# A decode step of a hybrid decoder on one core: layer norm statistics read from PSUM, and the second output projection gathered into eight split products

## The reference

```
layer 0:  h = rms_norm(x);  a, b, z = split(h @ w_in, 3)      # 3 x 2048 channels
          u = a * sigmoid(b);  c = causal depthwise conv, width 31, + bias
          c = silu(layer_norm(c) )                            # over 2048 channels
          x = x + (c * silu(z)) @ w_out0
          x = x + sigmoid(x @ gate_w[0]) * (p[0] @ ple_w[0])
shared:   k, v, logf from x;  k normed per head; 16 heads of 64
layer 1:  q, z from x;  o = softmax(q k^T + forget bias) v     # prompt: causal over 1024 keys
          x = x + (o * silu(z)) @ w_out                        # decode: 8 x 4096 cached keys by page table
          x = x + sigmoid(x @ gate_w[1]) * (p[1] @ ple_w[1])
```

## Time and profile before

| | |
|---|---|
| device time, median of 3 runs | 2558.25 us (2555.23 to 2560.53) |
| profiled execution, its own time | 2548.34 us, span 2546.5 us, mean TensorE clock 0.954 |
| convolution, layer norm | to 646 us, 646 to 776 us |
| slots | 1683 to 2382 us |
| rest of the projection | 2382 to 2418 us |
| `ple(1)` and the store | 2418 to 2546.5 us |

### The profile page before, as it was taken

The page is one execution under the profiler, slowest core; times in us unless marked ns, Lnnn a source line. Parts: engine busy times, 40 slices in busy tenths (PEclk is TensorE's granted clock), DMA queues, the critical chain, the costliest instruction groups (busy, mean ns, idle before and its releaser), DMA issues.

```text
span 2546.5 us, 44564 instructions
## 1 busy us (share of the span) xinstructions
PE 2284.5 (90%) x15044; PEld 1844.7 (72%) x15044; DVE 1390.6 (55%) x1990; ACT 949.7 (37%) x1622; POOL 1145.8 (45%) x802
## 2 busy tenths in 40 slices
PE   5999999997449998979999899877999999999799
PEld 4999999997249998969888686634454545545399
DVE  4789988899791016566785211023545455454523
ACT  4556655655351013223332121323343443434311
POOL 0798889988563214444445332232232232222211
PEclk7999999999669998989999999988999999999999
DMA  3222222222033121135635788899999999997312
GB/s 110 73 73 67 72 80 64 73 74 70 18 114 123 45 89 53 65 126 163 182 138 182 258 280 295 287 361 365 387 347 349 349 360 363 357 360 277 117 48 81
DMA packets 143702, 464.36 MB, mean 182 GB/s; under 512 B 28001, under 2 KB 36578, under 8 KB 142386
## 3 DMA queue, kind: packets, MB, share of 16 engines
q1 hardware_dynamic: 117954, 384.07, 43.2%
q0 software_dynamic: 22848, 62.56, 7.4%
q10 hardware_dynamic: 2736, 15.60, 1.5%
HBM read 403.58 MB, written 60.65 MB: 182 GB/s over the span
## 4 chain that ended last, share of the span: by engine, by line
PE 53%; POOL 12%; DVE 11%; issue 8%; DMA 8%; ACT 5%; SPq 2%; ACTq 0%; POOLq 0%; DVEq 0%
POOL ACC L1385 7%; PE PS L610 5%; PE PS L608 5%; PE PS L609 5%; PE PS L703 4%; PE PS L826 4%; PE PS L769 4%; PE PS L705 4%; PE PS L704 4%; PE PS L910 4%; DMA KV<-ck 3%; DMA KV<-cv 3%; PE PS L921 2%; PE PS L895 2%; PE PS L616 2%
## 5 line engine op out<-in xcount | busy, mean ns | idle before, releaser
L1358 POOL TENSOR_TENSOR WL<-RAW,WH 128x1024 fp32r<-128x1024 f32 (+1 forms) x113 | 283.6, 2510 | 454.4 <-ACT WH L995 447.9
L1710 DVE SCALAR_TENSOR_TENSOR PS<-UX,CWT,PS 128x1024 f32<-128x1024 f32 (+1 forms) x672 | 466.3, 784 | 0.0
L641 PE MATMUL PS<-HH,WH 128*128 128x384 f32 (+1 forms) x1152 | 378.9, 329 | 20.7 <-DVE HL L1696 20.7
L643 PE MATMUL PS<-HH,WL 128*128 128x384 f32 (+1 forms) x1152 | 377.8, 328 | 0.0
L642 PE MATMUL PS<-HL,WH 128*128 128x384 f32 (+1 forms) x1152 | 377.6, 328 | 0.0
L703 PE MATMUL PS<-GH,WH 128*128 128x384 f32 (+1 forms) x792 | 272.4, 344 | 29.8 <-DVE KC L1820 16.2
L1385 POOL TENSOR_TENSOR ACC<-ACC,PROD 128x1088 f32<-128x1088 f32 x112 | 284.7, 2542 | 31.3 <-ACT PROD L1047 25.1
L705 PE MATMUL PS<-GH,WL 128*128 128x384 f32 (+1 forms) x792 | 263.5, 333 | 0.0
L704 PE MATMUL PS<-GL,WH 128*128 128x384 f32 (+1 forms) x792 | 262.6, 332 | 0.0
L641 PEld LDWEIGHTS PS<-HH,WH 128*128 128x128 f32 x1152 | 217.6, 189 | 24.7 <-issue 13.7
L1602 POOL DMA_DIRECT2D QI<-qX_scr x128 | 77.7, 607 | 326.4 <-PE PS L879 324.9
(11 more groups left out here) (224 smaller groups left out, 4667.8 us busy)
## 6 DMA issues: line engine op xcount, KB each, us to landing
KV<-ck SPq DMA_DIRECT2D x256, 512.0 KB, 6.7
KV<-cv SPq DMA_DIRECT2D x256, 512.0 KB, 6.4
RAW<-wA SPq DMA_DIRECT2D x48, 512.0 KB, 3.6
RAW<-wP SPq DMA_DIRECT2D x16, 640.0 KB, 3.8
zT_scr<-ZS ACTq DMA_DIRECT2D x16, 544.0 KB, 2.7
Z<-zT_scr SPq DMA_DIRECT2D x16, 544.0 KB, 3.6
RAW<-wB SPq DMA_DIRECT2D x17, 512.0 KB, 3.7
RAW<-wO SPq DMA_DIRECT2D x16, 512.0 KB, 3.6
```

The source lines that it names most:

```text
L641: pe.matmul(out, WH[w][:, kk], HH[:, k, a:b], start=k == 0, stop=False)
L643: mm = pe.matmul(out, WL[w][:, kk], HH[:, k, a:b], start=False, stop=k == KD - 1)
L1358: pool.tensor_tensor(WL[s][:, 0:n], RAW[s][:, 0:n], WH[s][:, 0:n].bitcast(F32), ALU.subtract).then_inc(s_lo, 1)
L1710: i = dve.scalar_tensor_tensor(out=o, in0=x, scalar=w[:, j:j + 1], in1=o, op0=ALU.mult, op1=ALU.add)
```

## The change

Layer norm: the matrix of ones sums CSUM straight into the three PSUM banks of `CHAIN`; DVE subtracts the mean with one scalar_tensor_tensor that reads CHAIN, the inverse deviation is written to CHAIN, and the multiplication reads it there. ACT's copy of the mean goes.

Output projection: `out_product`, `out_add`, `load_wo`, WOF and the separate decode product go. The gated outputs of all pairs are kept in `OPA` (8 blocks of 1088 columns, the decode columns written by `sample_gated`), split into `OH` (ACT) and `OL` (DVE) behind the last slot, and multiplied in eight units `U_W` of 72 matmuls, whose weights go the usual way of `RAW`, `hi` and `lo`. Two of them are prepared in slots 120 and 122. X3 is read back behind the slots, at a new place; the load of `PR` (the embedding rows of layer 1, 1088 KB) waits for the last unit, since PR lies where OH was.

```diff
         X2 = Map(at_x)("X2", [P, KD, R])
-        X3 = Map(at_h)("X3", [P, KD, R])
+        X3 = Map(at_x)("X3", [P, KD, R])
...
+        OPA = Map(at_h)("OPA", [P, PAIRS, R])
+        OL = Map(at_h)("OL", [P, PAIRS, R], F32R)
+        OH = Map(at_h + 4 * KD * R)("OH", [P, PAIRS, R], F32R)
...
# SP
+            def raw_out(m):
+                u = U_W + m
+                sp.wait_ge(s_lo, u - 1)
+                sp.dma_start(RAW[u % 2][:, 0:KD * P].rearrange("p (k n) -> p k n", n=P),
+                             wW[:, :, P * m:P * m + P].rearrange("k p n -> p k n")).then_inc(s_raw[u % 2], 16)
             for g in range(2, N_STEPS):
                 pages(g)
+                if g == N_STEPS - 8:
+                    sp.wait_ge(s_s, 16 * (PAIRS - 1))
+                    raw_out(0)
+                    raw_out(1)
...
-            sp.wait_ge(s_ou, 16 * DB - 15)
+            sp.wait_ge(s_dd, N_STEPS)
+            sp.wait_ge(s_oz, 1)
+            sp.dma_start(X3[:], xS).then_inc(s_xs, 16)
+            for m in range(2, KD):
+                raw_out(m)
             ple_loads(1, U_TAIL)
...
# TensorE
-            colsum(pe, 0, CSUM).then_inc(s_mmu, 1)
+            pe.wait_ge(s_c, NCH)
+            for a, b in ((0, 512), (512, 1024), (1024, R)):
+                mm = pe.matmul(CHAIN[:, a:b], ONES, CSUM[:, a:b], start=True, stop=True)
+            mm.then_inc(s_mmu, 1)
...
-                    if c == 0:
-                        atleast(pe, s_po, x + 1 - 16)
-                    else:
+                    if c > 0:
...
-                if b > 0:
-                    out_product(b, t)
...
-            for u in range(2 * KD):
...
-                pe.matmul(PS[:, 3 + u % 4, :], WOP[:, P * (u // 2):P * (u // 2) + P],
-                          OP[1][:, 512 * (u % 2):512 * (u % 2) + 512], start=True, stop=True).then_inc(s_ou, 1)
...
-            ple(1, U_TAIL, (s_po, 16 * DB), (s_y, 1))
+            for m in range(KD):
+                u = U_W + m
+                pe.wait_ge(s_lo, u + 1)
+                atleast(pe, s_y, m - 1)
+                group(pe, m % 2, u % 2, OH, OL, KD, ready=s_ol if m == 0 else None).then_inc(s_unit, 1)
+            ple(1, U_TAIL, (s_y, KD - 1), (s_y, KD))
...
# ACT
-            for r, (a, b) in enumerate(RCH):
-                i = act.activation(MU[:, a:b], bank(0, r)[:, 0:b - a], ACT.Copy, scale=1.0 / EA)
-            i.then_inc(s_mu, 1)
...
-                if x == 3:
-                    act.wait_ge(s_unit, U_TAIL - U_OUT)
-                    act.dma_start(X3[:], xS).then_inc(s_xs, 16)
+                if x in (N_SLOTS - 8, N_SLOTS - 6):
+                    weights_out(U_W + (x - N_SLOTS + 8) // 2)
             prompt_evac(N_SLOTS - 1)
+            for k in range(PAIRS):
+                act.wait_ge(s_o, NQ * (k + 1))
+                act.wait_ge(s_oz, 1)
...
+                act.activation(OH[:, k, :], OPA[:, k, :], ACT.Copy).then_inc(s_oh, 1)
+            for m in range(KD):
+                if m < KD - 2:
+                    weights_out(U_W + m + 2)
+                if m == KD - 2:
+                    hi(U_TAIL, U_TAIL // 2 - PAIRS, U_TAIL % 2, SLOT)
+                act.wait_ge(s_y, m + 1)
+                act.activation(PLE_T[1][1][:, m, :], X3[:, m, :], ACT.Copy).then_inc(s_xh, 1)
+            act.wait_ge(s_unit, U_TAIL - U_OUT)
             act.dma_start(PLE_T[1][3][:], pT[1]).then_inc(s_prin, 16)
...
# POOL: load_wo and the WOF loads go
             pool.dma_start(ZSM[:], gT[:, :, SEQ:R].rearrange("a p n -> p a n")).then_inc(s_zsm, 16)
+            lo(U_W, U_W % 2)
             pool.wait_ge(s_o, NQ * DB)
+            for u in range(U_W + 1, U_TAIL):
+                lo(u, u % 2)
+            lo(U_TAIL, U_TAIL % 2, SLOT)
             p_lo(1)
...
# DVE
-                dve.tensor_tensor(CC[:, n, :], CC[:, n, :], MU[:], ALU.subtract).then_inc(s_xc, 1)
+                dve.scalar_tensor_tensor(out=CC[:, n, :], in0=CHAIN, scalar=-1.0 / EA, in1=CC[:, n, :], op0=ALU.mult,
+                                         op1=ALU.add).then_inc(s_xc, 1)
             dve.wait_ge(s_sd1, 1)
-            dve.reciprocal(MU[:], MU[:]).then_inc(s_inv, 1)
+            dve.wait_ge(s_xc, NCH)
+            dve.reciprocal(CHAIN, MU[:]).then_inc(s_inv, 1)
...
-                    dve.tensor_tensor(T1[n % 2][:], CC[:, n, :], MU[:], ALU.mult).then_inc(s_t1, 1)
+                    dve.tensor_tensor(T1[n % 2][:], CHAIN, CC[:, n, :], ALU.mult).then_inc(s_t1, 1)
...
-                dve.tensor_tensor(OP[par][:, c], PS[:, 7, 0:P], ZP[par][:, c], ALU.mult).then_inc(s_o, 1)
+                dve.tensor_tensor(OPA[:, b, c], PS[:, 7, 0:P], ZP[b % 2][:, c], ALU.mult).then_inc(s_o, 1)
+            def sample_gated():
+                dve.wait_ge(s_zsm, 16)
+                dve.wait_ge(s_os, DB)
+                dve.tensor_tensor(OPA[:, :, SEQ:R], OS[:], ZSM[:], ALU.mult).then_inc(s_oz, 1)
+            def o_lo(k):
+                dve.wait_ge(s_oh, k + 1)
+                dve.tensor_tensor(OL[:, k, :], OPA[:, k, :], OH[:, k, :].bitcast(F32), ALU.subtract).then_inc(s_ol, 1)
...
+            sample_gated()
+            for k in range(3):
+                o_lo(k)
             prompt_o(PAIRS - 1, NQ - 1)
+            for k in range(3, PAIRS):
+                o_lo(k)
...
+                    dve.wait_ge(s_unit, U_W + m + 1 - U_OUT)
+                    for r, (a, b) in enumerate(RCH):
+                        i = dve.tensor_tensor(X3[:, m, a:b], bank(m % 2, r)[:, 0:b - a], X3[:, m, a:b], ALU.add)
+                    i.then_inc(s_y, 1)
```

More of the change, by code:

```diff
@@ L225, in build @@
         assert m.at <= at_c
[L226 to L229, removed]
+        KX = [Map(at_r)("KX0", [P, 2, SEQ], F32R), KX1]
+        m = Map(at_r + 4 * SLOT * 4)
+        ZP.append(m("ZP1", [P, SEQ]))
         VP = [m("VP0", [P, NQ, P]), VP1]
-        ZP.append(m("ZP1", [P, SEQ]))
+        OPA = Map(at_h)("OPA", [P, PAIRS, R])
+        OL = Map(at_h)("OL", [P, PAIRS, R], F32R)
+        OH = Map(at_h + 4 * KD * R)("OH", [P, PAIRS, R], F32R)
         m = Map(at_r + 6 * SLOT * 4)
@@ L235, in build @@
         OE = m("OE", [P, 2 * HD])
[L237 to L240, removed]
         s_con, s_pt = sem("con_in"), sem("ptab_in")
@@ L253, in build @@
         s_slot, s_eva = sem("slot_mm"), sem("slot_copied")
-        s_mmu, s_mu, s_xc, s_sq1, s_var, s_sd1 = (
-            sem(x) for x in ("mu_mm", "mu", "xc", "sq1", "var_mm", "sd1"))
+        s_mmu, s_xc, s_sq1, s_var, s_sd1 = (
+            sem(x) for x in ("mu_mm", "xc", "sq1", "var_mm", "sd1"))
         s_sqp = sem("sq1_pairs")
@@ L273, in build @@
         s_fpo = sem("new_bias_out")
-        s_q, s_wo = [sem(f"keys_in{s}") for s in range(2)], [sem(f"wo_in{s}") for s in range(2)]
+        s_q = [sem(f"keys_in{s}") for s in range(2)]
         s_qi = [sem(f"queries_in{s}") for s in range(3)]
@@ L289, in build @@
         s_zsm = sem("silu_z_in")
-        s_wof, s_oz, s_ys, s_yc, s_yt, s_y = (
-            sem(x) for x in ("wof_in", "oz", "ys_mm", "ys", "ys_t", "x3"))
+        s_oz, s_y = sem("oz"), sem("x3")
         s_braw, s_end = sem("masks_in"), sem("y_out")
@@ L678, in unit @@
                     pe.wait_ge(*(free_gate if first else (s_sgp, KD * l + m)))
-                    group(pe, 0, (u0 + s) % 2, xh, xl, KD, ready=s_xl if first and l == 0 else None,
+                    group(pe, 0, (u0 + s) % 2, xh, xl, KD, ready=s_xl if first else None,
                           base=KD * l).then_inc(s_gate, 1)
@@ L897, in prompt_transpose @@
                     mm.then_inc(s_trp, 1)
[L899 to L911, removed]
             def prompt_pv(b, i):
@@ L1102, in _ @@
             for r, (a, b) in enumerate(RCH):
-                i = act.activation(MU[:, a:b], bank(1, r)[:, 0:b - a], ACT.Sqrt, scale=1.0 / EA,
+                i = act.activation(MU[:, a:b], bank(0, r)[:, 0:b - a], ACT.Sqrt, scale=1.0 / EA,
                                    bias=CST[:, C_EPS:C_EPS + 1])
@@ L1319, in prompt_evac, with weights_out @@
                     act.activation(PT[x % 2][:, a:e], PS[:, 5 + c, 0:e - a], ACT.Copy).then_inc(s_ev, 1)
+            def weights_out(u):
+                hi(u, u // 2 - PAIRS, u % 2)
             for i in range(T_UNITS, T_UNITS + T_LEAD):
@@ L1613, in load_z @@
                 pool.dma_start(ZP[b % 2][:], gT[b, :, 0:SEQ]).then_inc(s_zp[b % 2], 16)
-            def load_wo(b, part):
-                half = slice(4 * P * part, 4 * P * part + 4 * P)
-                pool.dma_start(WOP[:, half], wW[b, :, half]).then_inc(s_wo[part], 16)
             past_bias_at = {}
@@ L1647, in _ @@
                     load_bias(b + 1)
-                if t == 0 and b > 0:
-                    atleast(pool, s_ou, x - 16)
-                    load_wo(b - 1, 1)
                 if x > 0 and t % 2 == 0 and x // 2 + 2 < NQ * PAIRS:
```

117 lines of the change are left out of this document (26 added, 91 removed).

## The result

The changed kernel takes 2542.78 us (median of 4 runs, 2540.97 to 2543.75) where the kernel before, run beside it, takes 2556.74 (2555.05 to 2560.53): a ratio of 0.9944, with a 95% interval of 0.9929 to 0.9958. So it is 14 us faster. Run once more among the experiments it stood at 2547.18 against 2555.67, ratio 0.9961 (0.9947 to 0.9975), 8.5 us faster. The prediction was 2562, slower by 4, with 0.32 on faster: the time lies inside its range and on the other side of its forecast, towards rival A.

A forecast was written before the change was run, and what follows sets the result against it. TensorE and the page transfers were taken as two close limits, TensorE the bound by a little. Terms -18 - 39 + 61 = +4 us on the profiled 2548.3, plus 9.9 to the timed median, gave 2562 us, range 2536 to 2582.

The forecast's parts named there:

- rival A: Slots: page stream runs nearer its best rate, decisive from 370 GB/s; at 380 the kernel takes 2538 us; chance 0.27.
- The layer norm: Operands in PSUM relieve DVE in the last loop, and ACT's copy goes: 18 us gained, 1 to 30.
- the relief of the squares with the copy: Layer norm before its last loop: 2 us from four rounds of squares, 1.2 us from ACT's copy of the mean.
- Rival C: Layer norm's last loop: z multiplication and POOL still collide, POOL sets the loop; only 3 us gained, 2577; chance 0.07.
- The slots: Page stream sets the pace, 223.4 MB at 365 GB/s: 33 us, plus 6 at the end; 39 gained, 25 to 72.
- The 6 us at the end of the slots: From the last page's landing to the slots' end, 37 us before: the last slots lose their products, about 6 us gained.
- Behind the slots: Eight units on TensorE in 97 us, then `ple(1)` in 126 plus a 2.5 us stall: 61 us lost, 57 to 70.
- rival D: Behind the slots: the load of PR lands late, 8 us more, 2570 in all; chance 0.10.

The follow-up runs named there:

- four others: Traces: layer norm's part alone, changed kernel again, layer norm's part with X3 in blocks, changed kernel with two unit products of three; 2532.62, 2547.18, 2530.97, 2514.52 us.
- products out: Kernel before without the 112 output projection products in the slots and their additions, all loads kept; 2514.74 us, ratio 0.9842.
- both out: Kernel before without the products, their additions and their loads but for the last pair's weight, X3 filled with zeros; 2497.30 us, ratio 0.9775.
- the four and the five traces: Slots in four traces with the changed projection, mean 654.0 us, and in five with the projection as before, mean 700.6 us.

## Why the prediction was wrong, step by step

**The layer norm**: mechanism right, term 18, measured 21.5 timed, 19.6 in the trace of the changed kernel and 22.5 to 23.4 in four others. The bound of the loop was POOL (3.51) and not DVE (3.65), and the relief of the squares with the copy was mis-sized: 7 us rather than 3.2. Rival C named the right bound, as the z multiplication still collides with POOL, but its gain of 3 us is far off, since POOL at 3.5 us was not what set the 4.56 before.

**The slots**: this is the step that failed. That the page stream would set the pace was right, and its volume too. "I take 365", the mean of three windows of full share, was wrong: two of the three, at 356 and 369, were cut from a time in which TensorE was busy for 97 and 94% and still held the stream back now and then, though the share read 1.01. The third, the first pair with TensorE at 70%, read 370. Freed, it ran at 373 (changed kernel), 370 (its repetition, below), 376 (products out) and 374 GB/s (both out). The prediction itself named 370 as the point from which rival A decides; the 380 that A was priced at wasn't reached. With 373 in the prediction's own sum the slots gain 52 us, and the change comes out 9 us faster instead of 4 slower.

```profile
1680.00:2285.00 605.00, 520.28 (x4891) 287.41 (x4884) 243.50 (x638) 260.21 (x632) 167.93 (x293) 0.94 1.02 370
2285.00:2322.00 37.00, 26.53 (x190) 17.67 (x187) 19.39 (x41) 15.55 (x32) 5.50 (x6) 0.76 0.13 43
```

8 GB/s on 223.4 MB are 13 us. The 6 us at the end of the slots, taken as gained, were not; TensorE's clock, at 0.84 and here 0.76 there, may be part of the reason. The term was 39; measured are 46 and 40 us in the traces of the changed kernel against the 695.6 us of before's own, and 46.6 between the means of the four and the five traces. The term's lower bound, 25, doesn't follow from its parts, 21 + 6 = 27; nothing rests on it.

**Behind the slots**: term 61, measured 59.7 in the changed kernel and in its repetition (224.2 us both), and rival D falls: PR landed in 4.8 us, 5.1 being the estimate, and the stall was 0.5 us and not 2.5, which is most of the difference. That the mean duration of a matmul, 0.33 us, isn't its price was the most costly thing to get right here; it would have made the units 95 us longer.

**From the trace to the timed runs**: the sum of the terms as the traces show them is 2540.3 - 2546.5 = -6 us, +4 predicted: 7 us from the slots, 2 from the layer norm, 1 behind the slots. The rest lies in the level. I added 9.9 us to get from the profiled execution of before to its timed median, as though both kernels had this distance. But the changed kernel's profiled execution, 2542.1, is at its own median. The timed runs of before spread over 15 us, and its trace is of an execution faster than any of them. Against the medians the layer norm gives -21.5 and the projection +13.1, so its slots save some 47 us there and not 39 (60 - 13.1), which is also what the means of the traces say. The shift and the slots are thus one matter: before's trace has slots 5 us shorter than the mean of the five traces that share them, and the prediction took this stream of 645 us as the start of its sum and then added 9.9 us to both kernels alike. What makes one execution's slots longer than another's by up to 10 us stays open.

## What to carry to other kernels

Where two limits stand close together, the rate of the hidden one can't be read from the mean of windows, even of full share. A window in which the other limit is far off is a better guide, here the first pair with 370 GB/s, against 370 to 376 once the products had gone; better still is a run with the other limit taken away. Moving work from a place where it shares time with transfers to one where it stands alone has to pay its full throughput price, here 60 us for 47 saved; the part that paid took one of two SBUF inputs from a few DVE operations beside POOL. And a sum of terms from one profiled execution is good to no more than that execution's distance from the median, which should be in the range and not in the sum. Traces of variants that share a stage tell how far that stage scatters.

## What was not expected of the hardware

TensorE's granted clock fell in the last 34 to 37 us of the slots wherever the products had left them: to 0.84 (TensorE busy 23.1 of 34 us) and 0.76 (26.5 of 37) in the changed kernel and its repetition, and to 0.88 (27.6 of 36, 25.5 of 34) with the products, and with products and loads, out. In the kernel before it was 1.00 (30.6 of 37). 24 weight loads then take 2.43 us instead of 1.29. And the DMA share of a window reads 1.02 at 370 to 376 GB/s as well as 1.01 at 356: above 1.0 it doesn't order windows by how full they are. Last, DVE and POOL both pay when they collide: the splitting of OPA has two SBUF inputs and takes 1.28 us with POOL idle, and 3.50 at the most beside POOL's one operation, which itself takes 3.39 us instead of 2.41.
